# The first slot of weights in four pieces, and zeros on TensorE until the rows land

## The reference, cut to what matters

```python
D_MODEL = 1024
SEQ = 256
RMS_EPS = 1e-6

def rms_norm(x, gain):
    xf = x.astype(jnp.float32)
    y = xf * lax.rsqrt(jnp.mean(xf * xf, axis=-1, keepdims=True) + RMS_EPS)
    return (y * gain.astype(jnp.float32)).astype(x.dtype)

def first_block(x, ...):
    for l in range(DEPTH):
        h = rms_norm(x, norm_attn_pre[l])
        (a_q, a_kv, a_g, b_qkv, c_qkv, c_f, d_qlat, d_kvlat, d_krope) = split_cols(h @ w_in[l], IN_SPLITS)
        ...
```

## Time and profile before

| | |
|---|---|
| median of three runs | 1703.13 us (1700.63 to 1704.39) |
| the profiled execution | 1705.0 us |
| its span, first to last instruction | 1703.2 us |
| TensorE, share of the span | 96% |
| VectorE, ScalarE, GpSimd | 61%, 50%, 1% |

### The profile page before, as it was taken

One profiled execution on the slowest core, in us unless ns is written; L12 is line 12 of the kernel. 1 busy time (PEld: TensorE's weight loads), 2 busy tenths in 40 slices (PEclk: granted clock), 3 DMA queues, 4 the chain that ended last, 5 costly groups with the idle time before them and its releaser, 6 DMA issues.

```text
span 1703.2 us, 20946 instructions
## 1 busy us (share of the span) xinstructions
PE 1632.2 (96%) x8484; PEld 1380.6 (81%) x8484; DVE 1035.3 (61%) x1405; ACT 856.8 (50%) x1179; POOL 23.6 (1%) x26
## 2 busy tenths in 40 slices
PE   7988988999999999999899999999999999999999
PEld 7876876899987888877677888888888877778887
DVE  5554748688846554579766555455554765765553
ACT  4364655666635444444555544354443554664442
POOL 0000002000000000000000000000000000000000
PEclk9988988999999999999999999999999999999999
DMA  7746324455554555544042655555454432525553
GB/s 266 289 149 209 144 99 149 161 186 185 180 191 173 174 195 179 187 155 168 8 172 99 235 185 186 186 181 188 179 192 178 193 124 82 191 107 190 178 193 124
DMA packets 42961, 289.96 MB, mean 170 GB/s; under 512 B 5049, under 2 KB 5199, under 8 KB 9969
## 3 DMA queue, kind: packets, MB, share of 16 engines
q1 hardware_dynamic: 38272, 271.93, 44.0%
q0 software_dynamic: 4592, 16.69, 2.8%
HBM read 287.51 MB, written 8.55 MB: 174 GB/s over the span
## 4 chain that ended last, share of the span: by engine, by line
PE 86%; DVE 8%; ACT 2%; DMA 2%; issue 1%; DVEq 1%; SPq 0%; POOL 0%; ACTq 0%
PE bank L459 25%; PE bank L461 25%; PE bank L460 25%; PE bank L465 6%; DVE low L427 2%; DMA raw<-stream_dram 2%; PE bank L729 2%; PE bank L1338 1%; ACT high L416 1%; PE bank L1649 1%; DVEq L2568 1%; DVE stat L647 1%; DVE u L995 0%; PE bank L611 0%; PE bank L1845 0%
## 5 line engine op out<-in xcount | busy, mean ns | idle before, releaser
L427 DVE TENSOR_TENSOR low<-raw,high 128x2048 fp32r<-128x2048 f32 x255 | 583.0, 2295 | 376.3 <-ACT high L416 375.2
L416 ACT ACTIVATE high<-raw 128x2048 fp32r<-128x2048 f32 x257 | 488.8, 1913 | 373.3 <-DMA raw<-stream_dram 364.4
L459 PE MATMUL bank<-high,xh 128*128 128x512 f32 (+1 forms) x1232 | 486.2, 395 | 6.3 <-DVEq L2568 2.9
L461 PE MATMUL bank<-high,xl 128*128 128x512 f32 (+1 forms) x1232 | 478.2, 388 | 0.0
L460 PE MATMUL bank<-low,xh 128*128 128x512 f32 (+1 forms) x1232 | 477.4, 388 | 0.0
L459 PEld LDWEIGHTS bank<-high,xh 128*128 128x128 f32 x1232 | 232.5, 189 | 54.4 <-issue 4.2
L461 PEld LDWEIGHTS bank<-high,xl 128*128 128x128 f32 x1232 | 232.2, 188 | 48.3
L460 PEld LDWEIGHTS bank<-low,xh 128*128 128x128 f32 x1232 | 232.7, 189 | 44.7
L459 PE MATMUL bank<-high,hh 128*128 128x512 f32 x440 | 171.9, 391 | 0.0
L461 PE MATMUL bank<-high,hl 128*128 128x512 f32 x440 | 171.3, 389 | 0.0
L460 PE MATMUL bank<-low,hh 128*128 128x512 f32 x440 | 171.2, 389 | 0.0
(11 more groups left out here) (234 smaller groups left out, 1546.4 us busy)
## 6 DMA issues: line engine op xcount, KB each, us to landing
raw<-stream_dram SPq DMA_DIRECT2D x257, 1024.0 KB, 4.8
band_wide_dram<-band_rows_dram POOLq DMA_DIRECT2D x1, 3072.0 KB, 28.3
t_wide_dram<-t_rows_dram POOLq DMA_DIRECT2D x1, 2304.0 KB, 14.7
u<-mem_dram POOLq DMA_DIRECT2D x2, 1024.0 KB, 5.3
bias<-band_wide_dram POOLq DMA_DIRECT2D x1, 2048.0 KB, 15.0
rel_wide_dram<-rel_rows_dram POOLq DMA_DIRECT2D x1, 1920.0 KB, 15.6
bias<-t_wide_dram POOLq DMA_DIRECT2D x1, 1536.0 KB, 9.1
bias<-rel_wide_dram POOLq DMA_DIRECT2D x1, 1280.0 KB, 7.0
```

Source lines behind the costliest of these rows:

```text
L416: act.activation(self.high[:, n % RING, :], self.raw[:, n % RING, :], ACT.Copy).then_inc(self.high_split, 1)
L427: dve.tensor_tensor(self.low[:, n % RING, :], self.raw[:, n % RING, :], self.high[:, n % RING, :].bitcast(F32), ALU.subtract).then_inc(sel ...
L459: pe.matmul(out, lh, rh, start=start, stop=False)
L461: return pe.matmul(out, ll, rh, start=False, stop=stop)
```

## The change

Slot 0 is no longer one transfer of 1 MB but four of 256 KB (`PIECES = 4`), each with a semaphore of its own. The order in SyncE's queue becomes: identity, gains, left half of the rows, piece 0, right half of the rows, pieces 1, 2 and 3, and then slot 1 and the rest as before. ScalarE and VectorE split slot 0 piece by piece: piece 0 between the two halves of the rows, pieces 1 to 3 behind the right half. TensorE waits for a piece of slot 0 at every fourth piece of weights. GpSimd writes zeros into a 128 x 256 float32 tile at the start, and TensorE runs plain float32 matmuls of 256 columns on it: six ahead of the left half of the rows, two ahead of the right half, and two ahead of tile 0.

```diff
+PIECES = 4
...
+    def piece_cut(self, j):
+        return slice(j * SLOT // PIECES, (j + 1) * SLOT // PIECES)
+
+    def first_high(self, act, j):
+        act.wait_ge(self.piece_loaded[j], 16)
+        cut = self.piece_cut(j)
+        act.activation(self.high[:, 0, cut], self.raw[:, 0, cut], ACT.Copy).then_inc(self.piece_high, 1)
+        if j == PIECES - 1:
+            self.act_next = 1
+
+    def first_low(self, dve, j):
+        dve.wait_ge(self.piece_high, j + 1)
+        cut = self.piece_cut(j)
+        i = dve.tensor_tensor(self.low[:, 0, cut], self.raw[:, 0, cut], self.high[:, 0, cut].bitcast(F32), ALU.subtract)
+        i.then_inc(self.piece_low if j < PIECES - 1 else self.low_split, 1)
+        if j == PIECES - 1:
+            self.dve_next = 1
...
-        if i % m.per == 0:
+        if m.first == 0 and i < (PIECES - 1) * m.per // PIECES:
+            if i % (m.per // PIECES) == 0:
+                pe.wait_ge(self.piece_low, i * PIECES // m.per + 1)
+        elif i % m.per == 0 or (m.first == 0 and i == (PIECES - 1) * m.per // PIECES):
             pe.wait_ge(self.low_split, m.slot(i) + 1)
...
         self.rows(sp, 0)
+        self.piece(sp, 0)
+        self.rows(sp, 1)
+        for j in range(1, PIECES):
+            self.piece(sp, j)
+
+    def piece(self, sp, j):
+        c = self.core
+        cut = c.piece_cut(j)
+        sp.dma_start(c.raw[:, 0, cut], c.stream[0][:, cut]).then_inc(c.piece_loaded[j], 16)
+
+    def warm(self, pe, n):
+        c = self.core
+        pe.wait_ge(c.warm_ready, 1)
+        zeros = c.square[:, 0, 0:S]
+        for _ in range(n):
+            mm(pe, c.bank[1][:, 0:S], zeros[:, 0:P], zeros, True, True)
...
+    WARM = (6, 2, 2)
...
+        pool.memset(c.square[:, 0, 0:S], 0.0).then_inc(c.warm_ready, 1)
         pool.wait_ge(s["out_taken"], 2)
...
         for half in range(2):
+            self.first.warm(pe, self.WARM[half])
             self.first.wait_rows(pe, half)
             self.source.tensor(pe, s, half * KT // 2, (half + 1) * KT // 2)
+        self.first.warm(pe, self.WARM[2])
...
         self.source.highs(act, s, 0, KT // 2)
-        self.core.split_high(act, -LEAD)
+        c.first_high(act, 0)
         self.source.highs(act, s, KT // 2)
-        self.core.split_high(act, 1 - LEAD)
+        for j in range(1, PIECES):
+            c.first_high(act, j)
+        c.split_high(act, 1 - LEAD)
         self.source.scalar_norms(act, s)
...
             first.left(sp)
-            for n in range(core.act_next):
-                if n == 1:
-                    first.rows(sp, 1)
+            for n in range(1, core.act_next):
                 if n == 2:
                     first.tables(sp)
```

More of the change, by code:

```diff
@@ L390, in __init__ @@
         sem = nc.alloc_semaphore
+        self.piece_loaded = [sem(f"piece_loaded{i}") for i in range(PIECES)]
+        self.piece_high, self.piece_low, self.warm_ready = sem("piece_high"), sem("piece_low"), sem("warm_ready")
         self.slot_loaded = [sem(f"slot_loaded{i}") for i in range(RING)]
@@ L409, in over @@
         return self.nc.alloc_sbuf_tensor_at(name, shape, dtype, offset=at)
+    def piece_cut(self, j):
[13 more added lines that the diff above has]
+            self.dve_next = 1
     def split_high(self, act, last):
         for n in range(self.act_next, min(last + LEAD, self.slots - 1) + 1):
-            act.wait_ge(self.slot_loaded[n % RING], 16 * (n // RING + 1))
+            act.wait_ge(self.slot_loaded[n % RING], 16 * (n // RING + (n % RING > 0)))
             act.activation(self.high[:, n % RING, :], self.raw[:, n % RING, :], ACT.Copy).then_inc(self.high_split, 1)
@@ L421, in split_low @@
         for n in range(self.dve_next, min(last + LEAD, self.slots - 1) + 1):
-            dve.wait_ge(self.high_split, n + 1)
+            dve.wait_ge(self.high_split, n)
             if n in self.unsplit:
@@ L888, in vector @@
         self.source.lows(dve, s, 0, KT // 2)
-        c.split_low(dve, -LEAD)
+        c.first_low(dve, 0)
         self.source.lows(dve, s, KT // 2)
+        for j in range(1, PIECES):
+            c.first_low(dve, j)
         c.split_low(dve, 1 - LEAD)
```

## The result

The changed kernel is slower: 1708.21 us median of 7 runs (1705.6 to 1709.23) for 1703.13 of 7 (1700.24 to 1705.3), ratio 1.0029, 95% interval 1.0018 to 1.004. The forecast was 1700.6 with a range to 1704.6, and a chance of 0.09 for slower. The same two kernels measured once more gave 1.0026 (1.0015 to 1.0037). Two executions of the kernel before, of 2759 and 3300 us, are left out of all means and ratios. The profiled execution took 1708.21 us, its span 1706.4.

The account below looks back on a forecast made before the run. TensorE, busy 96% of the span, was taken to bound the kernel. Tiles 0 and 1 end 4.6 us sooner, a 2.1 us wait leaves 2.5 us: 1703.13 to 1700.6, range 1698.4 to 1704.6.

Parts of the forecast that it names:

- what is late next: First stage: `row` needs `wide_ready`, VectorE's spread copy, ending at 19.40 before and taken at 19.8 (19.40 to 20.9).
- The cap of 3.0 us: At `row`: TensorE can't pass before 19.40, so at most 22.42 - 19.40 = 3.0 us can be won.
- Zeros: Start: tile ready at 1.3, six calls take 5.0 us, hidden before the rows land; level rises at 7.4.
- Rows and piece 0: Start of the queue: a piece takes 0.66 us, so the rows' right half lands 2.0 us sooner, 8.85 for 10.84.
- I take the same speed: Slot 0's pieces were assumed to move as fast as the rows' right half, read at 445 GB/s.
- the row of 445 GB/s: Trace reading taken as the speed of the rows' right half, 2 KB rows as in a piece.
- Rival D: Small transfers at a third of the rate: slot 1 lands 5.3 us later, `wide_ready` at 24.8; 1708.5, chance 0.07.
- rival A: Clock falls in the new 2.1 us gap ahead of `row`, costing 3.0 us: 1703.6, chance 0.15.
- The bracket: The 2.1 us wait at `row` lies between 2.33 us (clock fell, 94.28) and 1.83 us (clock stayed, 165.14).
- Later waits go from stage to stage and move along: After the first stage: later waits shift with its end, so the 2.5 us gain reaches the end of the run.
- B: Gain given back later in the stage, as the stream's transfers land when they did: 1703.1, chance 0.10.

Follow-up runs that it names:

- e7_best: Kernel before plus matmuls on zeros at the start (slot 0 in one transfer), 20 matmuls in the wait near 94 and 16 near 852; ratio 0.9981.
- e2_zeros_only: Kernel before plus the same matmuls on zeros (6, 2, 2), slot 0 still in one transfer; ratio 0.9996.
- e10_fill_both: Changed kernel with seven matmuls on zeros ahead of the rows' left half, five ahead of the right half, and seven more ahead of `row`; ratio 1.0018.
- e12_after_again: The changed kernel itself measured once more, against the kernel before; ratio 1.0026.
- e1_no_zeros: Changed kernel without the matmuls on zeros and the clearing of their tile, the four pieces kept; ratio to the kernel before 1.0016.
- e3_fill_gap: Changed kernel with seven more matmuls on zeros between tile 1 and `row`; ratio to the kernel before 1.0004.
- e5_after_pad: Changed kernel with eight empty instructions on VectorE and eight on ScalarE at the start of the first stage; ratio to the kernel before 1.0033.

## Why the prediction was wrong, by its own steps

**What decides, "what is late next": right.** TensorE waited at `row` for VectorE's copy, which started at 20.35 and ended at 20.64, inside the bounds 19.40 to 20.9 and 0.8 us later than the 19.8 taken. The cap of 3.0 us held within 0.3: the earliest `row` of all kernels is at 19.18 (e7_best), where slot 1's `high` starts at 12.80 for 13.30.

**Zeros: right, a little too dear.** The tile was ready at 1.1 (1.3), the twelve instructions took 4.79 us (5.0), the clock rose near 5 us (7.4), the first product stood at 11.16 (11.8).

**Rows and piece 0, "I take the same speed": wrong.** I misread the row of 445 GB/s that I went by the earlier trace rows: 72 of its 95 packets are of 8 KB, and slot 0 had landed at 9.49, so they are slot 1's. The rows' right half itself moved at 403, but behind a large transfer. With slot 0 in four pieces the queue moved 302 GB/s over 5 to 10 us, 386 in two, 408 in one. It made slot 1 1.2 us late, and `row` 1.4 us later than in e2_zeros_only (20.78 for 19.41). The Trainium skill ("DMA: Bandwidth & Descriptors", section "Bandwidth"), by which smaller transfers get less bandwidth, was right in its direction; the trace agrees, by a quarter here.

**Rival D: its time came, its mechanism didn't.** D gave 1708.5, and 1708.21 was measured. That is luck: in D slot 1 lands 5.3 us later and `row` passes 22.42. It landed 1.2 us later, and `row` was sooner than before in every kernel.

**The gap, rival A: the first step that failed; its chance was put at 0.15.** The sum took the products behind `row` at the high level, and the cost of the wait ahead of it at nothing. I placed the wait of 2.1 us between one of 2.33 that was followed by a fall and one of 1.83 that wasn't, and argued that dense work ahead would save it. In seven of seven traces it didn't. The bracket itself was one trace's: at the place of the 1.83 us the clock fell in seven of the other traces, behind a wait of 1.81 us in e2_zeros_only and of 1.78 in e10_fill_both. The length of the last wait alone doesn't decide. The wait ahead of `row` was also longer in most, 2.0 to 3.5 us, as tiles 0 and 1 ended early and, with four pieces, slot 1 came late. Both go one way: the more the change won ahead of `row`, the longer the wait there. The price of A in the first stage was about right: with 6.8 us of low level (e12_after_again) the issue of slot 5's transfer moved from 30.16 to 31.45 although `row` was 1.4 us sooner, 2.7 us in all for 3.0. The rule of the Trainium skill that I had quoted for A ("TensorE: Matmul & The Clock Gate", section "HAM oscillation — how this bites in real kernels"), that waits between bursts throttle the array and the next burst starts slow, is what these traces show; the waits of its example are 3 to 5 us long, and here 2.0 to 3.5 were enough.

**"Later waits go from stage to stage and move along": the second step that failed, and its cause is in part open.** A and B both ended at the time of before. The rest is some 3 us. By means, 2.9 us of the changed kernel's loss go with the lower clock. Two things that I had taken as fixed moved.

The first is the stage's last transfer. It took 5.6 us for 4.7 in the profile, and between 4.7 and 7.0 over the traces. What goes with it is the instruction packet shown above: in nine traces it starts within 0.6 us of the transfer's issue, and the transfer takes 4.9 to 7.0 us (5.9 on average); in the other eight it comes elsewhere, and the transfer takes 4.7 to 5.0. The packet comes the earlier, the more matmuls stand ahead: at 59.3 without the zeros (e1_no_zeros), at 53.0 with them, at 51.8 and 50.5 with seven and eleven more (e3_fill_gap, e10_fill_both). So the zeros seem to move it onto the issue; no run moves it alone.

The second is the stage of the late place. There 0.25 us more idle time, in a stage that wasn't touched, goes with a low stretch of 3.4 us in five of the seven traces with four pieces and no filling there. In a sixth (e12_after_again) the same wait is followed by none, the seventh (e10_fill_both) is low from earlier on, and no trace without the delay has one. What makes VectorE's second instruction late in eight of the ten kernels with four pieces (in the other two the clock is already low there), and in none of the others, is open. How the 3 us divide isn't settled either: no pair of runs here separates the two beyond its interval.

**Forecasting by one profile.** The 2.5 us of gain were judged against a noise of about 1 us in a median. Much of the noise is itself the clock, and the change acted on it.

## What to carry to other kernels

Work that is moved ahead of a fixed wait lengthens that wait. If TensorE is the engine that then idles, ask first what the clock does behind 2 to 3 us without work, and fill the wait with matmuls on something harmless before judging the rest: with four pieces the second stage started 3 us sooner on average with it than without (61.3 to 62.6 against 63.5 to 66.8). In the time of the whole run less of that was seen, 1.0004 to 1.0018 for 1.0026 to 1.0029. And compare the mean granted clock of many runs, not one trace: a change can lower it in a stage that it doesn't touch.

## What the runs showed of the hardware that was not expected

- Matmuls on zeros in plain float32 raise the clock like others: the transposes from 5.98 already ran at the high level (1.09 us for 1.97).
- A wait of 2.0 us right behind dense products was enough for a fall (e5_after_pad: idle 2.02 ahead of `row`, granted clock low from 21.3). But no length parts the waits that take the clock from those that don't: near 165 one of 1.83 us left it high, and those of 1.81 and 1.78 us in e2_zeros_only and e10_fill_both were followed by 3.4 us of low level.
- The recorded clock says nothing before its first change: it prints 1.00 from 14 to 19.7 in the kernel before, where the products' pitch is that of the low level.
- A 1 MB load in four transfers for one moved a quarter less at the start of the queue: 302, 386 and 408 GB/s over 5 to 10 us with slot 0 in four, two and one. Packets of 2 KB as such reached 403.
- A transfer of the stream whose issue met a 16 KB instruction packet on another queue took 5.9 us on average for 4.9 (nine traces and eight).
- Runs of one and the same kernel differ by up to 10 us of 1705, and 0.001 of mean granted clock goes with 1.17 us.
